# Three norms of a decoder layer, made k-tile by k-tile

## What is computed

```python
mod = silu(c) @ w_ada + b_ada                       # one row per sequence: 9 of them
sh_a, sc_a, g_a, sh_c, sc_c, g_c = split(mod, 6)
h = rmsnorm(x, norm_mix_g) * (1 + sc_a) + sh_a      # norm 1
z = h @ w_in
x = x + g_a * (concat(rwkv7(z), mlstm(z)) @ w_out)
h = rmsnorm(x, norm_ffn_g) * (1 + sc_c) + sh_c      # norm 2
x = x + g_c * peer_ffn(h)                           # h @ w_q, keys, top 16 of 128, gates,
                                                    # gelu(h @ u) * gates @ v over 16384 experts
y = rmsnorm(x, norm_final_g) * (1 + scale) + shift  # norm 3
```

## Time and profile before

| what | value |
|---|---|
| time, median of 3 runs | 2950.87 us (2944.64 to 2962.13) |
| profiled execution, its own time | 2960.08 us |
| its span | 2958.3 us, mean granted TensorE clock 0.952 |
| busy: TensorE, weight loads | 2732.6 us (92%), 2622.4 us (89%) |
| busy: GpSimd, VectorE, ScalarE | 1756.1 us (59%), 1155.4 us (39%), 947.3 us (32%) |
| DMA | 544.93 MB, mean 184 GB/s |

### The profile page before, as it was taken

How to read it: one execution, slowest core, us unless ns; L and a number is a source line. 1 busy time by engine, 2 the same in 40 slices (tenths; PEclk the granted TensorE clock), 3 DMA queues, 4 the chain that set the end, 5 groups by cost and what they waited for, 6 DMA issues and landing times.

```text
span 2958.3 us, 62587 instructions
## 1 busy us (share of the span) xinstructions
PE 2732.6 (92%) x25895; PEld 2622.4 (89%) x25895; DVE 1155.4 (39%) x2200; ACT 947.3 (32%) x1315; POOL 1756.1 (59%) x723
## 2 busy tenths in 40 slices
PE   5689999988875979999999999999999999999997
PEld 3489998767763979999999999999999999999997
DVE  0360563554337650897477313200131101445133
ACT  1243442122112233444333333333332333222233
POOL 0167772003211757688655677787777777777774
PEclk9699997679996989999999999999999999999999
DMA  9634445887764434344444444454444545454442
GB/s 369 229 141 170 157 166 203 300 287 264 247 220 161 156 115 158 127 162 164 170 182 177 173 159 169 178 190 179 173 162 165 191 183 193 161 180 165 164 160 100
DMA packets 150177, 544.93 MB, mean 184 GB/s; under 512 B 8952, under 2 KB 18824, under 8 KB 120968
## 3 DMA queue, kind: packets, MB, share of 16 engines
q1 hardware_dynamic: 136384, 505.18, 47.7%
q10 hardware_dynamic: 11480, 20.44, 1.8%
q0 software_dynamic: 2160, 17.03, 1.5%
HBM read 518.77 MB, written 23.84 MB: 183 GB/s over the span
## 4 chain that ended last, share of the span: by engine, by line
issue 33%; POOL 31%; PE 26%; DVE 5%; DMA 3%; ACT 1%; POOLq 0%; SPq 0%; ACTq 0%; DVEq 0%
POOL ring_lo L583 31%; PE bank L658 25%; DMA kept<-in_w_ada 3%; DVE staged L1700 1%; DVE staged L1645 1%; DVE staged L1998 1%; ACT hi_front L1266 0%; PE bank L661 0%; POOLq L582 0%; DVE staged L1659 0%; ACT staged L1266 0%; DVE staged L1951 0%; DVE act_lo L2138 0%; POOLq L587 0%; DVE act_hi L2136 0%
## 5 line engine op out<-in xcount | busy, mean ns | idle before, releaser
L583 POOL TENSOR_TENSOR ring_lo<-kept,hi_peer 128x1024 fp32r<-128x1024 f32 x576 | 1443.6, 2529 | 535.7 <-ACT hi_peer L1266 535.6
L1266 ACT ACTIVATE hi_peer<-kept 128x1024 fp32r<-128x1024 f32 x576 | 578.2, 1052 | 1239.7 <-PE bank L658 1239.6
L658 PE MATMUL bank<-h_hi,ring_lo 128*128 128x288 f32 x3104 | 913.4, 294 | 0.0
L658 PE MATMUL bank<-h_hi,hi_peer 128*128 128x288 f32 x2304 | 685.7, 298 | 20.3 <-DVE h_lo L1674 15.1
L658 PE MATMUL bank<-h_lo,hi_peer 128*128 128x288 f32 x2304 | 680.4, 295 | 0.0
L658 PE MATMUL bank<-act_hi,hi_peer 128*128 128x288 f32 x2048 | 608.2, 297 | 17.6 <-POOL ring_lo L583 14.6
L658 PE MATMUL bank<-act_lo,hi_peer 128*128 128x288 f32 x2048 | 603.8, 295 | 0.0
L658 PE MATMUL bank<-act_hi,ring_lo 128*128 128x288 f32 x2048 | 603.6, 295 | 0.0
L658 PEld LDWEIGHTS bank<-h_hi,ring_lo 128*128 128x128 f32 x3104 | 585.7, 189 | 0.0
L658 PEld LDWEIGHTS bank<-h_hi,hi_peer 128*128 128x128 f32 x2304 | 432.4, 188 | 23.1 <-issue 18.5
L658 PEld LDWEIGHTS bank<-h_lo,hi_peer 128*128 128x128 f32 x2304 | 433.3, 188 | 0.0
(11 more groups left out here) (188 smaller groups left out, 2364.0 us busy)
## 6 DMA issues: line engine op xcount, KB each, us to landing
kept<-in_peer_u SPq DMA_DIRECT2D x128, 1024.0 KB, 4.8
kept<-in_peer_v SPq DMA_DIRECT2D x128, 1024.0 KB, 5.5
kept<-in_w_ada SPq DMA_DIRECT2D x96, 1024.0 KB, 8.7
kept<-in_w_in SPq DMA_DIRECT2D x50, 1024.0 KB, 4.8
kept<-in_w_adaf SPq DMA_DIRECT2D x32, 1024.0 KB, 5.5
kept<-in_w_out SPq DMA_DIRECT2D x16, 1024.0 KB, 4.8
kept<-in_w_q SPq DMA_DIRECT2D x16, 1024.0 KB, 4.7
gates_spill<-staged ACTq DMA_DIRECT2D x24, 576.0 KB, 3.0
```

The source lines that it names most:

```text
L583: pool.tensor_tensor(ring_lo[:, n % RING_SLOTS, cols], ring[n % RING_SLOTS][:, cols], hi_slot(n)[:, cols].bitcast(F32), ALU.subtract).then ...
L658: return pe.matmul(out, lhsT, rhs, start=start, stop=stop)
L1266: return act.activation(out, in_, ACT.Copy)
```

## The change

**Norm 1.** The scale row is now made first, the shift row second. Gain, reciprocal and the product x * gain * root of every k-tile are made before the shift row is there. The shift row is turned, stored and given its bias by quarters; for each quarter ScalarE adds the shift and rounds to the high part in one pass per k-tile, VectorE makes the low part in one scalar_tensor_tensor per k-tile, the samples follow in one operation, and TensorE runs the gates' part of this quarter. The gates use the split h and a split w_g (three fp32r products). The high part of the first w_in tile is made before the last quarter is taken, that of the second after all. `dense` waits for the split by quarters.

**Norm 2.** In the w_out stage ScalarE squares the new x1 k-tile, before it makes its high part of tile n+2, and VectorE adds the square before it waits for the next tile; the last square goes to the sum on TensorE by a matmul of its own. The reciprocal root is written to PSUM. VectorE multiplies rows k-tile by k-tile, in the order `XN_ORDER`; seven k-tiles (`H2_POOL`, 3 to 15 by twos) are shifted in place and get their low part on GpSimd, nine (`H2_DVE`) are shifted and rounded in one pass on ScalarE and get their low part on VectorE. GpSimd makes the low part of the first w_q tile before and those of the others after this work. `dense` of the w_q stage waits for the split every four k-tiles, on two semaphores.

**Norm 3.** The first eight k-tiles are squared by ScalarE within the last segment and added up by VectorE there; the ones matmuls are 9 for 16. A first root on a spare place stands ahead. VectorE multiplies row by row, ScalarE shifts the even and GpSimd the odd k-tiles, and y is stored in four quarters.

**Value tiles.** A v tile that is neither first nor last of a half waits for the first half of its low part, and for the second one ahead of its e = 1 matmuls.

Some semaphores are merged (exp, const, reloaded), which changes no order but that the aux loads are waited for earlier.

```diff
-        hi_front = [parts("hi_front0", M_ADAS, D), parts("hi_front1", q5, D)]
+        hi_front = [parts("hi_front0", q5, D), parts("hi_front1", M_ADAS, D)]
+        wg_hi, wg_lo = parts("wg_hi", za, KT, 36), parts("wg_lo", za + KT * 36, KT, 36)
-        ada_order = [SH_A, SC_A, G_A, SH_C, SC_C, G_C, SH_F, SC_F]
+        ada_order = [SC_A, SH_A, G_A, SH_C, SC_C, G_C, SH_F, SC_F]
@@ SyncE
+            for b in range(4):
+                sp.wait_ge(S("y_done_act"), 2 * b + 2)
+                sp.wait_ge(S("y_done_pool"), 2 * b + 2)
+                sp.dma_start(T["y"][:, 4 * b:4 * b + 4], yn[:, 4 * b:4 * b + 4]).then_inc(S("y_stored"), 16)
@@ GpSimd
-            lo_tiles(n_wo, n_end - n_wo)
+            lo_tiles(n_wo, KT)
+            lo(n_q)
+            for kt in H2_POOL:
+                h2_kt = h2[:, kt, 0:TP]
+                pool.wait_ge(S("xn_ready"), xn_made(kt))
+                pool.tensor_scalar(h2_kt, h2_kt, mods[:, SH_C, kt, 0:1], None, ALU.add).then_inc(S("pool_shift"), 1)
+                if kt > H2_POOL[0]:
+                    pool_low(kt - 2)
+            pool_low(H2_POOL[-1])
+            for j in range(1, RING_SLOTS):
+                lo(n_q + j)
+            lo_tiles(n_q + RING_SLOTS, n_end - n_q - RING_SLOTS)
...
+            for kt in YN_POOL:
+                pool.wait_ge(S("xn_ready"), KT + kt + 1)
+                pool.tensor_scalar(yn[:, kt, 0:TP], yn[:, kt, 0:TP], mods[:, SH_F, kt, 0:1], None, ALU.add
+                                   ).then_inc(S("y_done_pool"), 1)
@@ TensorE, prologue
+            for b in range(4):
+                for q in range(4):
+                    ada_step(1, b, q)
+                    if b and q == 0:
+                        shift_turn(b - 1)
+                    if b and q == 3:
+                        gate_part(b - 1)
+            shift_turn(3)
+            gate_part(3).then_inc(S("gates_ready"), 1)
@@ TensorE, dense
-                        if split:
-                            pe.wait_ge(S("act_split"), 2 * split - 1 + kt // 8)
+                    if split == "h2":
+                        if kt % 4 == 0:
+                            pe.wait_ge(S("act_split"), SPLIT_BASE["h2"] + 1 + sum(t < kt + 4 for t in H2_DVE))
+                            pe.wait_ge(S("pool_split"), sum(t < kt + 4 for t in H2_POOL))
+                    elif split and kt % SPLITS[split][0] == 0:
+                        pe.wait_ge(S("act_split"), SPLIT_BASE[split] + SPLITS[split][1] * (kt // SPLITS[split][0] + 1))
@@ TensorE, v_tile
-                pe.wait_ge(S("lo_ready"), i * 8 + (2 * dense_index(n) + 2))
+                both = first or last
+                pe.wait_ge(S("lo_ready"), i * 8 + (2 * dense_index(n) + 1 + both))
                 pe.wait_ge(S("acts_split"), i * 4 + acts_split_n(n) + 1)
                 for dt, e in turns:
+                    if not both and (dt, e) == (0, 1):
+                        pe.wait_ge(S("lo_ready"), i * 8 + (2 * dense_index(n) + 2))
@@ TensorE, end
-            norm_sum(ysq, 2 + KT, 0, KT, 1)
+            pe.wait_ge(S("y_half_sum"), 1)
+            matmul(ps[0][:, 0:N], ones, ysq[:, 0, :], True, False)
+            for kt in range(8, KT):
+                pe.wait_ge(S("squares"), 1 + KT + kt + 1)
+                mm = matmul(ps[0][:, 0:N], ones, ysq[:, kt, :], False, kt == KT - 1)
@@ ScalarE, prologue
+            for b in range(4):
+                if b == 3:
+                    hi(n_z)
+                if b == 0:
+                    ada_store(0)
+                ada_take(1, b)
+                kts = slice(4 * b, 4 * b + 4)
+                act.wait_ge(S("ada_turned"), 2 + b)
+                copy(mods[:, SH_A, kts].rearrange("p k s -> p (k s)"),
+                     ps[3][:, b * 4 * NS:(b + 1) * 4 * NS]).then_inc(S("mods_raw"), 1)
+                act.wait_ge(S("h_ready"), 2 * b + 1)
+                for kt in range(4 * b, 4 * b + 4):
+                    activate(h_hi[:, kt, 0:TP], hT[:, kt, 0:TP], ACT.Identity, bias=mods[:, SH_A, kt, 0:1]
+                             ).then_inc(S("act_hi"), 1)
+                act.wait_ge(S("h_ready"), 2 * b + 2)
+                copy(h_hi[:, kts, TP:N], hT[:, kts, TP:N]).then_inc(S("act_hi"), 1)
             hi(n_z + 1)
@@ ScalarE, w_out
                     act.wait_ge(used, i * 4 + (n_wo + j + 1))
+                    act.wait_ge(S("out_free"), i * 4 + (j + 3))
+                    activate(x1sq[:, 1 + j % 2, :], x1[:, bass.ds(i * 4 + j, 1)].rearrange("p o n -> p (o n)"), ACT.Square
+                             ).then_inc(S("x1_squared"), 1)
                     hi(n_wo + j + 2, i)
@@ VectorE, prologue, for each quarter b
+                tt(m, m, over(prm("bada", SH_A * KT + 4 * b, 4), 2, NS), ALU.add).then_inc(S("h_ready"), 1)
+                dve.wait_ge(S("h_ready"), 2 * b + 1)
+                tt(hs[:, kts], hs[:, kts], over(mods[:, SH_A, kts, 1:], 3, TS), ALU.add).then_inc(S("h_ready"), 1)
+                for kt in range(4 * b, 4 * b + 4):
+                    dve.wait_ge(S("act_hi"), HI_BASE["h"] + 5 * b + kt % 4 + 1)
+                    stt(out=h_lo[:, kt, 0:TP], in0=hT[:, kt, 0:TP], scalar=mods[:, SH_A, kt, 0:1],
+                        in1=h_hi[:, kt, 0:TP].bitcast(F32), op0=ALU.add, op1=ALU.subtract).then_inc(S("act_split"), 1)
@@ VectorE, norm 2
+            def h2_row(kt):
+                stt(out=h2[:, kt, 0:TP], in0=x1[:, kt, 0:TP], scalar=gain2[:, kt, 0:1], in1=ps[3][:, 0:TP],
+                    op0=ALU.mult, op1=ALU.mult).then_inc(S("xn_ready"), 1)
+            lows = list(H2_DVE)
+            for at, kt in enumerate(XN_ORDER):
+                h2_row(kt)
+                if at == 1:
+                    link(tt(h2[:, :, TP:N], h2[:, :, TP:N], over(ps[3][:, TP:N], 1, KT), ALU.mult))
+                    tt(h2s, h2s, over(mods[:, SH_C, :, 1:], 3, TS), ALU.add).then_inc(S("h_ready"), 1)
+                if at % 2 and at > 1:
+                    h2_low(lows.pop(0))
```

More of the change, by code:

```diff
@@ L753, in _ @@
                     pe.wait_ge(S("z_free"), i * 4 + (j + 1))
-                    dense(n_z + j, h_hi, h_lo, i, j % 2, 1)
+                    dense(n_z + j, h_hi, h_lo, i, j % 2, "h")
             with pe.Fori(0, 6) as i:
@@ L1351, in _ @@
             norm_root(rms, 1, 0)
-            ada_store(0)
-            for q in range(4):
-                ada_take(1, q)
-            ada_store(1)
-            hi(n_z)
+            act.wait_ge(S("aux_in"), 128)
+            copy(wg_hi, aux("wg", KT, 36)).then_inc(S("act_hi"), 1)
+            for b in range(4):
[14 more added lines that the diff above has]
+                copy(h_hi[:, kts, TP:N], hT[:, kts, TP:N]).then_inc(S("act_hi"), 1)
             hi(n_z + 1)
-            affine_split(hT, h_hi, gain, SH_A, 1)
-            act.wait_ge(S("aux_in"), 128)
             zqs = zq[:, :, TP + 3:ZQW].rearrange("p s (b t) -> p s b t", t=7)
@@ L1559, in _ @@
             for half in range(2):
-                split_hi(ymix, y_hi, half)
+                split_hi(ymix, y_hi, half, "y")
             with act.Fori(0, KT // 4) as i:
@@ L2152, in v_acts @@
                                 apply_gates(3, 2 * half + j // 8, j // 4 % 2)
+                    elif s == 7 and half == 1:
+                        for j in range(1, 16):
+                            split_acts(n1 + j, q, 2 * j)
+                            if j == 9:
+                                dve.wait_ge(S("squares"), 1 + KT + 8)
+                            if j >= 9:
+                                link(tt(ysq[:, 0], ysq[:, 0], ysq[:, j - 8], ALU.add))
+                        link(stt(out=gain3, in0=mods[:, SC_F], scalar=1.0, in1=over(prm("gfin"), 2, NS), op0=ALU.add,
+                                 op1=ALU.mult))
+                        dve.sem_inc(S("y_half_sum"), 1)
                     else:
@@ L2203, in _ @@
             dve.wait_ge(S("out_taken"), 64)
-            norm(xo, yn, rms3, gain3, SH_F, SC_F, "gfin", 3, S("y_done"))
+            yns = samp(yn)
+            link(tt(yns, samp(xo), over(gain3[:, :, 1:], 3, TS), ALU.mult))
+            dve.wait_ge(S("norm_root"), 3)
+            link(dve.reciprocal(ps[3][:, 0:N], rms3[:, 0, :]))
+            for kt in range(KT):
+                stt(out=yn[:, kt, 0:TP], in0=xo[:, kt, 0:TP], scalar=gain3[:, kt, 0:1], in1=ps[3][:, 0:TP],
+                    op0=ALU.mult, op1=ALU.mult).then_inc(S("xn_ready"), 1)
+                if kt == 3:
+                    link(tt(yn[:, :, TP:N], yn[:, :, TP:N], over(ps[3][:, TP:N], 1, KT), ALU.mult))
+                    tt(yns, yns, over(mods[:, SH_F, :, 1:], 3, TS), ALU.add).then_inc(S("y_done"), 1)
 OUTS = {
```

258 lines of the change are left out of this document (157 added, 101 removed).

## The result

The changed kernel takes 2921.89 us (median of 4 runs, 2909.46 to 2923.63). The kernel before, with one run more than the three shown ahead, has a median of 2956.5 us. The ratio is 0.9871 with a 95% interval of 0.9842 to 0.9899, so the change saves 38 us (30 to 47). The forecast was 2911 us, in a range of 2898 to 2927. The profiled execution went from a span of 2958.3 to 2919.9, which is -38.4 where the sum gave -40.2, and from 2960.08 to 2921.68 us, where the sum gave 2919.9.

The account below looks back on a forecast made before the run. TensorE, at work 92% of the span, was taken as the bound. Terms -15.0, 0, -7.5, -12.0 and -5.7 sum to -40.2, taking 2960.08 to 2919.9; less 9.2 for the median gives 2911 us, range 2898 to 2927.

Parts of the forecast that it names:

- What bounds it: Whole kernel: TensorE works 92% of the span; gains only where it stands still around a norm or misses its beat.
- Part 1: Prologue: first dense matmul at 124.2 instead of 140.0, less a cold-start cost; -15.0 us, bounds -12 to -18.
- Part 2: Out-projection: ScalarE's high parts come 1.6 us later but stay hidden, with 1.3 us to spare; 0 us.
- its rule: VectorE and GpSimd hold each other up; the form reading a PSUM bank and one SBUF tensor was never held.
- Part 3: Norm 2: first query matmul at 1075.8 against 1083.6, later k-tiles keeping up; -7.5 us, bounds -2 to -8.5.
- Part 4: Value tiles, segment 2: six of eight low-part waits of 2.0 us go; -12.0 us, bounds -9 to -13.
- Part 5: Tail: square sum done at 2937.4 instead of 2941.6, shorter path to last store; -5.7 us, between -4 and -7.
- The step from the profile to the median: Final time: the profiled execution stands 9.2 us above the three-run median, so 2919.9 becomes 2911 us.
- (a): Prologue and norm 2: holding by GpSimd eats the small pieces; -33.7 us in all, 2917 us; chance 0.08.
- (b): Value tiles: the stall moves instead of going; -28.2 us in all, 2923 us; chance 0.05.
- (c): Input projection, query and value tiles: 308 added waits break TensorE's stream, costing 58 us; 2969 us; chance 0.02.
- (d): Prologue: the ring stalls behind three gate parts between weight tiles, 8.7 us if unhidden; 2919 us total; chance 0.04.

Follow-up runs that it names:

- both experiments on this edit: Changed kernel with every value tile again waiting for both low-part halves: 2941.92 us, 0.9937; kernel before with only the value-tile wait edit: 2946.80 us, 0.9956.
- the tail's edit: Changed kernel with an early root table load, no wait for the last two tiles before the squares, all norm 3 shifts on ScalarE: span 2918.8 us.

## Why the prediction was right, step by step

**What bounds it** held: the gains lie where TensorE stood still, but for the 3 us of inner value tiles named under part 4. That the sum came within 1.8 us of the profile's 38.4 is in part luck: norm 2 and the tail were priced 3.1 and 1.7 us too high, the value tiles 2.9 too low.

**Part 1 (-15.0, measured -15.3)** was right in sum and in each step, down to the bias add held by GpSimd's first low part and the sample add by its second. What it took for given, the order on ScalarE and that on TensorE, was worth another 4.4 us, about half of it each, which it did not look for. The cold start cost less: the first 7.1 us of dense matmuls ran at a mean granted clock of 0.93, where I had argued from the 0.56 and 0.79 of the earlier trace rows. The row, with the clock third from the end:
```profile
124.20:131.30 7.10, 7.10 (x52) 7.10 (x51) 0.00 (x0) 0.00 (x0) 1.70 (x1) 0.93 0.00 0
```

**Part 2 (0)** held: ScalarE's high parts come 1.6 us later and are 6.35 us apart as before, in both kernels. The 10 us of y, which the prediction used as evidence for its rule, held 4.6 us that could be had; the change left them there.

**Part 3 (-7.5, measured -4.4)** is the most mis-sized term. The start of TensorE was right (-7.7). What failed is the sentence "I take 0.6" for GpSimd's operations on 256 columns: the shift takes 0.92 and the subtraction 0.73, so a k-tile takes 1.65 us for 1.2, seven of them 11.6 for 8.4 (12.9 in the trace, with what held them or let them wait), and "Later k-tiles come 0.6 us apart and keep up with the cold start" was false: the first query tile took 11.0 us from its first matmul to its release, where it took 8.35 before. The second took 7.0 for 6.35, as its low part came late. The k-tiles moved from GpSimd show it: with five the first tile is released 1.9 us earlier, and with the second tile's low part made ahead the second 2.6. The Trainium skill (GPSIMD Engine Reference, opening paragraph) calls VectorE roughly 2x faster at elementwise work; on 256 columns the traces have 0.92 against the 0.40 of VectorE's tensor_scalar where nothing held it (minimum and median of the row below, in the trace before), and 0.73 against the 0.42 of its tensor_tensor, 2.3 and 1.7 times, which roughly agrees. An estimate from the page's factor and these rows, 0.8 for either operation, would have given 1.6 us a k-tile, close to the 1.65 measured.
```profile
L1645 DVE TENSOR_SCALAR staged<-staged,kept x7: 400/406/2424, 123.6 to 133.0; 128x256 f32<-128x256 f32 x7
133.75 0.42 DVE L1665 TENSOR_TENSOR staged<-staged,kept 128x256 f32<-128x256 f32 x1
```

**Part 4 (-12.0, measured -15.3)** had the mechanism: six stalls, and the two last tiles of halves remain. The size of a stall was right too: of the 13.0 us in segment 2 some 0.8 are what each other segment gained, which leaves 2.0 for each of the six (the one low-clock tile stands in both traces and adds nothing to the difference). Missed were the 3 us of inner tiles that showed no wait, 2.3 in segments 0, 1 and 3 and 0.8 here; both experiments on this edit have them.

**Part 5 (-5.7, measured -4.0)** gave 4.2 us to the sum of squares, and 2.5 came: it assumed that the sum would end with TensorE's nine matmuls and missed that ScalarE's squares stand behind the last tile's release and the 1.28 us table load (2.0 us of idle TensorE, won back by the tail's edit), and again sized GpSimd's shifts at 0.6: the last store is issued 9.4 us behind the reciprocal's end, where 8.5 was forecast and 9.5 measured before. The stores went the other way: the end comes 3.2 us behind the last store's issue for 4.6, 1.4 us gained where 0.5 was counted on.

**The step from the profile to the median** was the weakest of all: 9.2 us were taken off because the profiled execution stood that far above a median of three. The next runs of the kernel before gave 2961.8 (14 runs) and 2960.98 (9 runs): the profiled 2960.08 was ordinary, the median of three low. Without this step the forecast reads 2919.9, and 2921.89 was measured.

**Rivals.** (a) held in the prologue, priced in already, and not in norm 2: the low rows took 0.57 us in the mean and not several. The Trainium skill (SBUF — State Buffer, two separate sides) locks the pair for one instruction. The traces agree with that for most held instructions and not for the first low part of y, which lost its turn at three ends in a row (last section). (b) fell: the waits went and did not reappear. (c) fell: 47 w_in tiles (2 to 48) take 310.09 us with two waits more each and 310.11 without them. (d) did not decide, since nothing was lost in sum, but its kind of cost appeared once the order was changed: a gate part of 2.65 us ahead of a turn.

## What to carry to other kernels

Price an operation on GpSimd by a row of that operation and size, not by a fraction of a longer one, and share work so that both engines finish together; here five k-tiles against eleven beat both seven and none. Where the trace shows a long VectorE instruction with two SBUF tensors held ahead of a start, try to hold GpSimd back for it: here a wait gained 4.6 us. And before taking a profiled execution to a median, ask how many runs the median has, since three of them were off by 10 us, a quarter of the whole gain.

## What the runs showed of the hardware

Three things were new to me. A held VectorE instruction does not always get its turn at the end of GpSimd's current one: the first low part of y waited over three such ends (10.08 us) and, with GpSimd held back, over one (5.47). It is the exception. In the trace of before the product of the first half of norm 1, of the same 128x2304 and from two SBUF tensors, began under GpSimd's first low part, which ended at 118.92, and was done at 121.33, 2.42 us later, although GpSimd's next instruction stood ready; that one took 4.67 us for some 2.35:
```profile
118.39 2.94 DVE L1659 TENSOR_TENSOR staged<-staged 128x2304 f32<-128x2304 f32 x1
118.87 4.67 POOL L583 TENSOR_TENSOR ring_lo<-kept,hi_front 128x1024 fp32r<-128x1024 f32 x1
```
The same holds for the split of 128x576 at 2684.95 in after (2.82 us for 0.76, one end) and for the three squares at 969.10, 1019.85 and 1045.24 in before (2.70 to 2.72 for 0.46, one end each). What sets the low part of y apart, no run shows. A scalar_tensor_tensor of 128x256 with one bank operand was never held (467 to 481 ns in 32 cases), and with two SBUF operands took up to 1012. And GpSimd's tensor_scalar is longer than its subtraction on the same 256 columns (922 against 729 ns), although it reads one tensor less.
